# Moving two PSUM copies and one set of transposes two ticks later in a two-layer block with gathered experts

## The reference

```python
for l in range(DEPTH):                       # 2 layers
    h = rmsnorm(x, norm_mix_g[l])
    p_conv, p_attn, p_ssm = split(h @ w_in[l])
    y = concat(rmsnorm(conformer_conv(p_conv)), rmsnorm(stick_breaking_attention(q, k, v)),
               rmsnorm(s5_ssm(p_ssm)))
    x = x + y @ w_out[l]
    x = x + memory_cross_attention(rmsnorm(x), rmsnorm(mem), ...)
    x = x + peer_ffn(rmsnorm(x), ...)        # 8 heads, 16 experts each, per token
return rmsnorm(x, final_norm_g)
```

## Time and profile before

| | |
|---|---|
| time, median of 3 runs | 1684.7 us (1683.33 to 1685.03) |
| the profiled execution | 1680.37 us, of which the profile's span is 1678.4 us |
| PE busy | 1533.3 us (91% of the span) |
| DVE busy | 1166.9 us (70%) |
| ACT busy | 745.2 us (44%) |
| POOL busy | 604.4 us (36%) |
| DMA | 669.87 MB, mean 399 GB/s, of which the gathers 536.90 MB |
| granted clock of PE | 0.987 of full speed on average |

### The profile page before, as it was taken

One profiled execution on the slowest core, in us unless ns is written; L12 is line 12 of the kernel. 1 busy time (PEld: TensorE's weight loads), 2 busy tenths in 40 slices (PEclk: granted clock), 3 DMA queues, 4 the chain that ended last, 5 costly groups with the idle time before them and its releaser, 6 DMA issues.

```text
span 1678.4 us, 19097 instructions
## 1 busy us (share of the span) xinstructions
PE 1533.3 (91%) x6334; PEld 892.5 (53%) x6334; DVE 1166.9 (70%) x2901; ACT 745.2 (44%) x2021; POOL 604.4 (36%) x527
## 2 busy tenths in 40 slices
PE   9999799999999999899989889999999998777776
PEld 8757575456567656444545446455655454222332
DVE  7821899856878658986555667985667666666655
ACT  4142534754365334484433353476445335333333
POOL 0000454333334334343333433333434454444442
PEclk9999999999999999999998999999999999999999
DMA  9646999999999999999999999999999999999997
GB/s 385 263 166 259 372 418 421 421 421 421 421 420 417 414 421 421 422 420 421 421 422 421 412 421 421 416 369 421 421 421 421 421 421 421 421 421 421 417 422 291
DMA packets 93282, 669.87 MB, mean 399 GB/s; under 512 B 10344, under 2 KB 10624, under 8 KB 12416
## 3 DMA queue, kind: packets, MB, share of 16 engines
q0 software_dynamic: 73728, 536.90, 77.3%
q1 hardware_dynamic: 19312, 131.49, 19.3%
q10 hardware_dynamic: 144, 0.26, 0.0%
HBM read 667.57 MB, written 1.05 MB: 398 GB/s over the span
## 4 chain that ended last, share of the span: by engine, by line
PE 41%; DMA 35%; DVE 14%; ACT 7%; issue 2%; POOL 0%; ACTq 0%; DVEq 0%; POOLq 0%
DMA slots<-expert_rows,expert 35%; PE bank L1001 17%; PE bank L472 9%; DVE slots L2055 6%; PE bank L675 4%; PE bank L984 3%; PE bank L968 3%; ACT diag L1533 1%; DVE sg L1582 1%; ACT coef L1555 1%; ACT L1550 1%; DVE products L1800 1%; PE bank L740 1%; ACT gel L1550 1%; ACT L1285 1%
## 5 line engine op out<-in xcount | busy, mean ns | idle before, releaser
L1001 PE MATMUL bank<-slots,diag 128*128 128x512 f32 x1902 | 899.1, 608 | 124.4 <-ACT diag L1533 121.7
L1151 POOL DMA_INDIRECT slots<-expert_rows,expert x512 | 602.5, 1177 | 1049.9 <-PE bank L1001 835.6
L2055 DVE CUSTOM_DVE_ANT_0 slots<-slots,htok 128x1024 f32<-128x1024 f32 x512 | 625.7, 1222 | 378.5 <-DMA slots<-expert_rows,expert 370.9
L1001 PEld LDWEIGHTS bank<-slots,diag 128*128 128x128 f32 x1902 | 345.0, 193 | 538.7 <-issue 326.5
L1550 ACT ACTIVATE gel<-dot 128x2 f32<-128x2 f32 (+1 forms) x258 | 52.5, 204 | 630.3 <-DVE dot L2055 629.7
L1533 ACT ACTIVATE diag<-ident,coef 128x128 f32<-128x128 f32 x476 | 167.3, 394 | 8.4
L472 PEld LDWEIGHTS bank<-hT,ring 128*128 128x128 f32 x1152 | 141.5, 195 | 32.1 <-issue 32.1
L472 PE MATMUL bank<-hT,ring 128*128 128x128 f32 x1152 | 141.8, 278 | 0.0
L1555 ACT ACTIVATE coef<-gel,gexp 128x1 f32<-128x1 f32 x512 | 123.0, 287 | 10.4
L1550 ACT ACT_TABLE_LOAD x70 | 89.8, 1283 | 1.2
L1582 DVE SCALAR_TENSOR_TENSOR sg<-htok,prm,sg 128x128 f32<-128x128 f32 x240 | 71.3, 341 | 0.0
(11 more groups left out here) (377 smaller groups left out, 1514.0 us busy)
## 6 DMA issues: line engine op xcount, KB each, us to landing
ring<-w_blocks SPq DMA_DIRECT2D x81, 1024.0 KB
slots<-w_blocks SPq DMA_DIRECT2D x22, 1024.0 KB, 13.5
slots<-expert_rows,expert POOLq DMA_INDIRECT x512
kept<-w_blocks SPq DMA_DIRECT2D x6, 1024.0 KB, 14.8
keys<-w_blocks SPq DMA_DIRECT2D x2, 1024.0 KB, 10.4
phasor<-w_blocks SPq DMA_DIRECT2D x2, 1024.0 KB
prm<-w_blocks SPq DMA_DIRECT2D x2, 1024.0 KB
kv<-w_blocks SPq DMA_DIRECT2D x2, 1024.0 KB, 12.6
```

The lines of the kernel that those rows point to most:

```text
L1001: last = mm(bank[h][:, :], diag[:, i % DIAGS, :], slots[:, SLOT[n], D + h * 512:D + (h + 1) * 512], start=m == 0, stop=n == end - (ph == N ...
L1151: nc.gpsimd.indirect_dma_start(slots[:, s, :], None, (experts0_d, experts1_d)[n // PER // NC], bass.IndirectOffsetOnAxis(ap=idx[q % 2][:, ...
L2055: v.tensor_tensor_reduce(out=slots[:, s, 0:D], in0=slots[:, s, 0:D], in1=htok[:, ph % 2, :], scale=1.0, scalar=0.0, op0=ALU.mult, op1=ALU.add,
```

## The change

It moves three kinds of steps, and adds or removes no operation.

1. In chunks 1 to 3 ACT copies the turned weights of groups 0 and 2 at step 7 in place of step 5, two ticks later. The copies of groups 1 and 3, and all of chunk 0, stay. Since the sigmoids of the next group write over what the transposes read, they get the wait for the transposes that the copy had until now.
2. PE's transposes of the late rows for head 4 (chunks 1 and 3) stand at tick 37 of the chunk in place of 35.
3. ACT's copies of them stand at tick 38 in place of 36.

PE's wait for the copy of "att t" keeps its place at step 6.

```diff
@@ late_queries on PE
-                        yield at + tick - 4
+                        yield at + tick - 2
@@ attention on ACT
+                def turned_in(g):
+                    name = ("att t", g, ci)
+                    src = full(name)[:, :].rearrange("p (h k s) -> p h k s", h=2, k=2)
...
+                    done(act(aTs[ci][:, g % 2, :, 0:1 + c, :], src[:, :, 0:1 + c, :], ACT.Copy), name)
+
                 for step_ in range(5):
                     g = step_ - 1
-                    if g >= 0:
+                    if g >= 0 and (g % 2 or ci == 0):
                         yield att_tick(ci, g, 5)
...
+                        turned_in(g)
                     g = step_
                     if g < 4:
                         yield att_tick(ci, g, 1)
...
+                        if g:
+                            full(("att t", g - 1, ci))
                         act(sns[ci][:, :, lo:S], src, ACT.Sigmoid, scale=-AD ** -0.5)
...
                     g = step_ - 1
+                    if g >= 0 and g % 2 == 0 and ci:
+                        yield att_tick(ci, g, 7)
+                        turned_in(g)
@@ late_queries on ACT
-                        yield at + tick - 3
+                        yield at + tick - 1
```

More of the change, by code:

```diff
@@ L1266, in attention @@
                     act(ahead[:, :], zero[:, :], ACT.Sigmoid)
+                def turned_in(g):
+                    name = ("att t", g, ci)
+                    src = full(name)[:, :].rearrange("p (h k s) -> p h k s", h=2, k=2)
+                    if g == 0 and ci:
+                        full(("ssm y", ci))
+                    if g >= 2:
+                        full(("att o", 0, ci))
+                    done(act(aTs[ci][:, g % 2, :, 0:1 + c, :], src[:, :, 0:1 + c, :], ACT.Copy), name)
                 for step_ in range(5):
                     g = step_ - 1
-                    if g >= 0:
+                    if g >= 0 and (g % 2 or ci == 0):
                         yield att_tick(ci, g, 5)
[L1271 to L1277, removed]
+                        turned_in(g)
                     g = step_
```

## The result

| | before | changed |
|---|---|---|
| median, 19 runs each | 1681.03 us (1679.84 to 1685.03) | 1685.01 us (1683.32 to 1689.87) |
| ratio, 95% interval | | 1.0020 (1.0013 to 1.0028) |
| the profiled execution, its span | 1680.37 us, 1678.4 us | 1688.48 us, 1686.5 us |
| PE, ACT busy | 1533.3 us, 745.2 us | 1535.9 us, 747.0 us |

The change costs 0.20%, 0.0020 x 1681 = 3.4 us (the medians are 4.0 us apart). The forecast was +0.5 us: the measured value lies in its range, but at the upper edge of what it called the same, and the interval reaches to both sides of that edge. That the forecast median of 1685.2 us lies 0.2 us from the measured 1685.01 is luck: it was built on a median of before of 1684.7 us from 3 runs, and 19 runs gave 1681.03.

What follows compares the result with a forecast made beforehand. The slowest DMA engine bounds the kernel from 200 us on, so PE's delays cost 0; a third of 1.5 us is allowed, +0.5: 1680.37 to 1680.9, with the runs' median 4.3 above, 1685.2 us; range 1681.5 to 1690.0.

Steps and rivals of the forecast that it cites:

- what it called the same: Whole kernel: about 0.2%, 3.4 us, taken as what a measurement can tell from no change; chance 0.68.
- the wait that did not move: PE's wait for ACT's copy: stops of some 3.8 us in chunk 3's group 0 and 2.5 us in group 2.
- The diagonals come earlier: Chunk 3, rival: diagonals begin 1.68 us earlier; removing stop and low clock would give 4.4 us, 1680.3; chance 0.09.
- The clock's 1.70 us a stop: PE behind a new stop: the 1.2 GHz level falls on later work and adds 1.70 us.
- Chunk 3's gap: 1106 to 1118 us, DMA share 0.79 at 272 GB/s: costs almost none, since the slowest engines are busy through it.
- The rival without the low clock: PE's clock doesn't fall behind the stops: delays of 1.5, 1.7 and -0.2 us, 1684.7 us; chance 0.03.
- within the first case: The hidden case: PE's delay stays hidden behind the slowest DMA engine, within 3.4 us of no change; chance 0.65.
- the cover for both delays: Group 2's gathers, chunks 1 to 3: 8.8 us at least of queue, above the 7.7 of both delays.
- 2.1 + 2.49: Each gather's own time in us: 2.1 from issue to data, 2.49 for the transfer at 420 GB/s.
- the delay of group 0 in chunk 1: PE behind group 0's stop: late by 1.5 us, or 3.2 with the low clock, against 5.3 to spare for gather 50.
- chunk 3's delay: PE behind group 0's stop in chunk 3: between 0.2 us early and 1.5 late, taken as 1.5.
- the gathers run dry: Rival: chunk 3's 1.5 us go straight to the end, chunks 1 and 2 lose 1.7 each; about 5, 1689.7; chance 0.23.

Runs made afterwards that it cites:

- chunk3_only: All three parts of the change in chunk 3 alone, chunks 1 and 2 as in the kernel before; ratio to before 1.0005, 1681.75 us.
- no_wait: The changed kernel, but in chunks 1 to 3 PE does not wait at step 6 for an even group's copy; ratio to before 1.0005, 1681.60 us.
- third_first: The changed kernel with PE's wait for an even group's copy one tick later, behind the third expert; ratio to before 0.9999, 1680.82 us.
- stops_attention: The kernel before plus four matmuls of zeros on PE at step 6 of groups 0 and 2, chunks 1 to 3; ratio 0.9998, 1681.01 us.
- filled_stop_3: The changed kernel plus three matmuls of zeros on PE ahead of each of the six waits for a copy; ratio to before 1.0003, 1681.47 us.
- chunks12_only: All three parts of the change in chunks 1 and 2 alone, chunk 3 as in the kernel before; ratio to before 1.0016, 1684.01 us.
- group0_only: The change for group 0 alone in chunks 1 to 3, with the late rows; group 2's copies as before; ratio to before 1.0006, 1683.57 us.
- late_only: The kernel before with only the late rows' transposes and copies two ticks later, turned weights' copies in their old place; ratio 1.0000, 1680.40 us.
- group2_only: The change for group 2's copies alone in chunks 1 to 3; group 0's copies and late rows as before; ratio to before 0.9993, 1681.04 us.

## Why the prediction was nearly right, and what it got wrong

**Right.** PE stops at the wait that did not move, six times and about as long as worked out (3.94 for 3.8, 2.57 for 2.5; in chunk 2 group 2's was 3.55 for the same 2.5, and group 0's 3.30 had no number of its own). The diagonals come earlier and it doesn't help. The clock's 1.70 us a stop is near the average of the six, 1.6. Chunk 3's gap is covered by the engines that run behind: chunk3_only deepens it to one engine at no measurable cost, and no_wait and third_first, whose rate there is 401 and 399 for 381, gain nothing. A delay of PE is covered by the queue up to a bound: stops_attention and filled_stop_3 cost nothing. The rival without the low clock, "within the first case", is what filled_stop_3 measured.

**Wrong: the cover for both delays.** The forecast set the 7.7 us of a chunk's two delays against "8.8 us at least" of queue and let them cost nothing. The delay was right: gather 184 is issued 7.8 us late in chunk 2. The queue of before was there too: gather 184 took 17.5 us from its issue to its dot, 12.9 without the 2.1 + 2.49 that the forecast calls its own. But with the change it took 7.1 us, which leaves 2.5 of queue and not 12.9 - 7.8 = 5.1. So the queue shrank by more than PE's delay, and the rate fell to 257 GB/s: some of the engines had run dry. The four kernels with this gather 7.4 to 9.2 us late paid; one group's stops alone did not measurably. Whether the slowest engine itself ran dry, which the forecast made the condition of any cost, is not shown: the gather after it has 1.3 us left by the same count (751.81 to 757.69), about the 1.2 that it called the error of such counting.

**Wrong: the delay of group 0 in chunk 1.** The forecast had the fourth expert 1.5 to 3.2 us late, with 5.3 to spare. It was 5.3 late: the low clock had 2.9 of that in place of 1.70, the rest 2.4 in place of 1.5. So nothing was left to spare. But this alone is not the price: chunks12_only, where the fourth expert is 4.2 us late, costs 0.0016, and group0_only, with 5.1 us, 0.0006.

**Wrong: which expert was looked at.** The working compared the ends of the blocks, the fourth expert and what follows. By the same numbers the third is late by more: in chunk 3, 1100.34 + 0.87 + 1.80 = 1103.0 against 1095.05 + 3.60 = 1098.65, 4.4 us. Its slot comes free behind the stop, and its gather is the first to be late; the expert itself is 6.5 us late in chunk 1. At full clock, 4.3 us of that are still covered (filled_stop_3), so this omission alone was not what cost; it hid how little room was left.

**The sum.** +0.5 us was a third of chunk 3's delay, but chunk 3 is where nothing measurable is paid. The price, 3.4 us, came from chunks 1 and 2, where the rival "the gathers run dry" had put most of its own. That rival had 5 us, with 1.5 of it wrongly in chunk 3, and chunks 1 and 2 at 1.7 each. That twice 1.7 gives the measured 3.4 is in part luck: it stood for what the low clock adds at one stop each, and the dots have 2.1 and 1.2.

**Open.** Chunks 1 and 2 lost 3.4 + 4.0 us of mean rate in the profiled execution, and the dots show 2.1 + 1.2 us paid. No view tells which of the sixteen engines ran dry, so how the one becomes the other stays open. In chunk 2 the rate falls behind both stops (276 GB/s from 727 to 730 us, 257 from 748 to 751). In chunk 1 it falls behind group 0's alone (246 GB/s from 319 to 322 us) and is back at 425 from 325 to 349 us, so that a chunk pays only for both stops is not shown there. Whether group 2's copies alone gain a little (0.9993) wasn't followed up.

No variant beats the kernel before: late_only and third_first are equal to it within their intervals.

## What to carry to other kernels

When the producer of a wait is moved, move the wait too: one tick on PE's side made the same change free. A delay on the engine that frees buffers is to be set, with the clock that PE will have behind the stop, against the time that the queue has in hand at that very place: at the first buffer that it holds back, and again behind a second stop, where the delays add up. A fall of the mean transfer rate is no measure of what is lost: 29 GB/s less over 55 us cost nothing that could be measured, 22 and 26 GB/s less over 65 us each at two other places came with 3.4 us.

## What was not expected of the hardware

Stops of the same length are not always followed by the same clock. In group2_only PE waits equally long for the same diagonals in chunks 1 and 3:

```profile
306.11 3.14 PE L1001 MATMUL bank<-slots,diag 128*128 128x512 f32 x4 [2.67 <-ACT diag L1541]
...
1106.80 1.99 PE L1001 MATMUL bank<-slots,diag 128*128 128x512 f32 x4 [2.66 <-ACT diag L1541]
```

The expert behind the first took 3.14 us, the one behind the second 1.99, at granted clocks of 0.63 (306 to 309 us) and 1.00 (1106 to 1109). The price of a stop can so be 1.2 us apart between two places, and, with the rest of the program a little shifted, between two kernels.
